# Two buffers for the scan's output matrices, and a new order of the work around layer norm's roots and the powers

## The reference, cut to what matters

```
mod = silu(cond) @ ada_w[i] + ada_b[i]              # shift, scale, gate, three groups of 2048
cn  = rmsnorm(ctx) * (1 + scale) + shift

def chunk_mixer(h):                                  # layer 0
    z = gelu(h @ w_in);  u, v = split(z)
    v = layernorm(v, ln_g, ln_b)                     # mean, squares, root, reciprocal
    return (u * (w_s @ v + b_s)) @ w_out

# layer 1: h[t] = a * h[t-1] + bb @ u[t],  y[t] = real(c @ h[t]), a, bb, c complex, 64 groups
mag = exp(lr * step);  a = mag * (cos, sin)(li * step)
bb  = ((a - 1) * conj(l) / |l|^2) * b
```

## Time and profile before

| | us |
|---|---|
| median of 3 runs | 3821.16 (3813.0, 3821.16, 3826.5) |
| profiled execution, its own time | 3819.04 |
| span of that execution in the trace | 3817.1 |
| first gather of the experts starts, from the span's start | 323.19 |

### The profile page before, as it was taken

How to read it: one execution, slowest core, us unless ns; L and a number is a source line. 1 busy time by engine, 2 the same in 40 slices (tenths; PEclk the granted TensorE clock), 3 DMA queues, 4 the chain that set the end, 5 groups by cost and what they waited for, 6 DMA issues and landing times. The chain is left out here.

```text
span 3817.1 us, 46785 instructions
## 1 busy us (share of the span) xinstructions
PE 3233.0 (85%) x15952; PEld 2126.1 (56%) x15952; DVE 2248.8 (59%) x5038; ACT 1428.4 (37%) x3564; POOL 972.1 (25%) x796
## 2 busy tenths in 40 slices
PE   3877999898889988986748888889769889799897
PEld 2765566454435555532436544444237789577797
DVE  5665667666666666687252576667632289212397
ACT  1222444444344444443242344444432166222265
POOL 0002434333334433444100354445520000000000
PEclk6888999999999999999878999999989999888899
DMA  6747999999999999999684799999952244221353
GB/s 247 284 171 289 421 411 420 421 411 419 420 397 411 410 414 415 413 395 361 272 292 146 294 421 421 421 421 420 410 240 79 79 178 159 116 83 69 126 187 118
DMA packets 177136, 1152.67 MB, mean 302 GB/s; under 512 B 21860, under 2 KB 30264, under 8 KB 43306
## 3 DMA queue, kind: packets, MB, share of 16 engines
q0 software_dynamic: 113936, 827.38, 53.0%
q1 hardware_dynamic: 56058, 304.90, 21.2%
q10 hardware_dynamic: 6944, 17.91, 1.2%
HBM read 1128.86 MB, written 21.25 MB: 301 GB/s over the span
## 5 line engine op out<-in xcount | busy, mean ns | idle before, releaser
L1126 PE MATMUL PS<-AR 128*128 128x512 f32 x3072 | 1508.7, 617 | 257.1 <-ACT AR L1184 248.7
L1311 POOL DMA_INDIRECT AR<-in_peer_uv,AR x768 | 959.0, 1249 | 1507.0 <-PE PS L1126 1097.5
L1287 DVE CUSTOM_DVE_ANT_0 AR<-AR,H 128x1024 f32<-128x1024 f32 x768 | 941.6, 1226 | 664.5 <-DMA AR<-in_peer_uv,AR 644.9
L1126 PEld LDWEIGHTS PS<-AR 128*128 128x128 f32 x3072 | 558.6, 193 | 862.9 <-issue 419.4
L1179 ACT ACTIVATE SM<-SM 128x1 f32<-128x1 f32 x768 | 155.4, 202 | 1152.9 <-DVE SM L1287 1151.7
L1087 PEld LDWEIGHTS PS<-HT,W 128*128 128x128 f32 x1536 | 296.8, 194 | 270.3 <-issue 255.1
L1087 PE MATMUL PS<-HT,W 128*128 128x256 f32 x1536 | 425.0, 385 | 2.7 <-issue 1.3
L1184 ACT ACTIVATE AR<-CON,SM 128x128 f32<-128x128 f32 x768 | 308.4, 402 | 40.3 <-PE PS L1126 15.3
L2576 PE MATMUL PS<-XP,WP 128*128 128x256 f32 x2112 | 264.2, 288 | 22.6 <-DVE WP L2733 15.7
L2576 PEld LDWEIGHTS PS<-XP,WP 128*128 128x128 f32 x2112 | 262.2, 196 | 26.3 <-issue 25.3
L1181 ACT ACTIVATE SM<-SM 128x1 f32<-128x1 f32 x768 | 226.4, 295 | 25.0
(11 more groups left out here) (368 smaller groups left out, 3391.2 us busy)
## 6 DMA issues: line engine op xcount, KB each, us to landing
W<-in_peer_w_q SPq DMA_DIRECT2D x48, 1024.0 KB
W<-in_ada_w SPq DMA_DIRECT2D x32, 1024.0 KB
W<-in_ffn_gate SPq DMA_DIRECT2D x22, 1024.0 KB
W<-in_ffn_val SPq DMA_DIRECT2D x22, 1024.0 KB
W<-in_ffn_out SPq DMA_DIRECT2D x22, 1024.0 KB
W<-in_cm_w_in SPq DMA_DIRECT2D x16, 1024.0 KB
AR<-min_scr SPq DMA_DIRECT2D x16, 1024.0 KB, 10.1
AR<-in_peer_uv,AR POOLq DMA_INDIRECT x768
```

The lines of the kernel that those rows point to most:

```text
L1126: mm = pe.matmul(PS[:, 4 + (u % 2) * 2 + c, :], self.DIAG[:, r % 4, :], self.UV[:, r % RING, D + c * 512:D + (c + 1) * 512], start=(k == 0 ...
L1287: v.tensor_tensor_reduce(rows_, rows_, H[:, self.tb(u), :], 1.0, 0.0, ALU.mult, ALU.add, self.ACTV[:, u % 2, k:k + 1]).then_inc(u_used.sem, 1)
L1311: g.indirect_dma_start(out=self.UV[:, r % RING, :], out_offset=None, in_=t["peer_uv"], in_offset=bass.IndirectOffsetOnAxis(ap=self.IDS[:, ...
```

## The change

The output matrices get a second buffer, at another place of the arena. The second half of `dve_powers` becomes a function of its own, `dve_powers_of`; the first half (a, the factors, bb) is called ahead of the bias of `ada0[0]`, the second half behind it. `act_roots` follows `act_squares`, ahead of `act_in(4)` and `matrices(2)`. ScalarE gets two waits: ahead of each MOUT store but the first for the store before, and ahead of the experts for the store of chunk 6, whose buffer lies where the experts' scores go. The numbers of steps between VectorE's other work are new.

```
-                self.MOUT = view(0, 2, CG, T8 * GDIM)
+                self.MOUT = [view(18432, 2, CG, T8 * GDIM), view(0, 2, CG, T8 * GDIM)]
...   act_store(c)
                 a.wait_ge(self.mout_done, c + 1)
-                a.dma_start(mout_scr[c], self.MOUT.rearrange("p r g x -> p (r g x)")).then_inc(self.mout_out, 16)
+                if c:
+                    a.wait_ge(self.mout_out, c * 16)
+                a.dma_start(mout_scr[c], self.MOUT[c % 2].rearrange("p r g x -> p (r g x)")).then_inc(self.mout_out, 16)
...   dve_powers
                 drain(self.cmul(self.BBR, self.BBI, over_c(self.CO_R), over_c(self.CO_I), self.BR, self.BI, self.T1, self.T2))
+
+            def dve_powers_of(self):
+                L, X1, X2, A_R, A_I, PR, PI = self.link, self.X1, self.X2, self.A_R, self.A_I, self.PR, self.PI
                 L(v.memset(PR[:, 0], 1.0))
...   dve
-                    MIN, CST, MOUT = self.MIN[c % 2], self.CST[c % 2], self.MOUT
+                    MIN, CST, MOUT = self.MIN[c % 2], self.CST[c % 2], self.MOUT[c % 2]
...
-                    if c:
-                        v.wait_ge(self.mout_out, c * 16)
+                    if c > 1:
+                        v.wait_ge(self.mout_out, (c - 1) * 16)
...   first_act
             mixc.act_squares()
+            mixc.act_roots()
             drain(mixc.act_in(4))
             matrices(2)
-            mixc.act_roots()
             drain(mixc.act_in(5))
...
+            a.wait_ge(prep.mout_out, 7 * 16)
             peer0.act(fill_act(), rest_of_matrices, first_block_norm())
...   first_dve
             drain(norm1c.variances())
+            prep.dve_powers()
             ada0[0].add_bias()
-            prep.dve_powers()
+            prep.dve_powers_of()
             matrices = prep.dve()
...
             drain(norm1c.apply())
-            some(40)
+            some(42)
             ada0[1].add_bias()
             mixc.dve_means()
-            some(2)
+            some(1)
             mixc.dve_vars()
-            some(2)
+            some(1)
             drain(mixc.dve_apply(0))
-            some(24)
+            some(30)
             ada0[2].add_bias()
-            some(6)
+            some(4)
             drain(mixc.dve_mix())
```

## The result

| | before | changed |
|---|---|---|
| median of 5 runs | 3824.28 (3813.0 to 3828.56) | 3795.97 (3785.51 to 3800.83) |
| profiled execution, its own time | 3819.04 | 3795.97 |
| span of that execution in the trace | 3817.1 | 3794.2 |
| first gather of the experts | 323.19 | 302.99 |

The forecast was 3798.5 in a range from 3790 to 3809: right in sign and in size. The times that follow are starts from the beginning of the span.

The account below looks back on a forecast made before the run. The prediction took TensorE's ordered list to bound the front and DMA transfers the experts' stretch from the first gather. Gains of 8.46 + 13.12 = 21.6 us gave 3797.5 on the profiled execution, 3799.6 by the median; it said 3798.5, range 3790 to 3809.

Parts of the forecast that it names:

- Part 1, 8.46: First norm on VectorE: with the powers split around the first bias, its application starts at 63.09, not 71.55, gaining 8.46 us.
- The worry about the rows' landing: First norm: the bias 3.08 late might delay the rows' load; landing 2 us later would cut the gain to 6.6.
- The wait of 7.85: TensorE at `prep.pe(3)`: its 7.85 us wait for VectorE's copy ending MIN(3) goes, with 12 us to spare.
- The clock's price, 4.91: `prep.pe(3)` on TensorE: without the wait it runs at the high clock, 6.62 us in place of 11.53.
- The block behind, 0.36: TensorE's block behind `prep.pe(3)`: takes 8.84 us in place of 9.20, gaining 0.36.
- Second buffer and early roots: VectorE and ScalarE before MIN(3): no store wait, roots at 144.1 in place of 164.1 (times of before), 20 us earlier.
- New waits at no cost: ScalarE's waits ahead of MOUT stores and the experts cost nothing; stores 17 us or more apart, 2.8 to spare at the experts.
- Sum, 21.6 at the first gather: Whole front: 8.46 + 13.12 = 21.6 us, putting the first gather at 301.6 in place of 323.19.
- rival (d): TensorE in the front: clock sinks at other places, each `prep` group costing 4.9 more; slower, up to 3831.8; chance 3%.
- signs of being wrong: TensorE's wait for L962 staying, a gather later than 306, or a stretch behind it longer by more than a few us.
- The rest unchanged at 3493.9: From the first gather to the span's end: the distance stays unchanged at 3493.9 us.

Follow-up runs that it names:

- powers_only: The kernel before with only the powers in two parts around the first bias; ratio to before 0.9979, 8.0 us less.
- before_again: The kernel before, unchanged, profiled a second time; first gather at 327.61 us, no ratio given.
- late_roots: The changed kernel with layer norm's roots back behind `matrices(2)`; ratio to before 0.9989, 4.2 us less.
- matrices_only: The changed kernel with the powers joined again behind the first bias; ratio to before 0.9972, 10.7 us less.
- min3_first: late_roots with two more steps of MIN(3) ahead of `dve_apply`, which finish that matrix; ratio to before 0.9970, 11.5 us less.
- after_again: The changed kernel, unchanged, measured and profiled a second time; ratio to before 0.9949, 19.5 us less.
- after_third: The changed kernel, unchanged, profiled a third time; first gather at 307.02 us, no ratio given.
- one_buffer: The changed kernel with a single output buffer again and the last step count between output blocks cut from 3 to 1; ratio to before 0.9976, 9.2 us less.
- roots_only: The kernel before with only layer norm's roots moved right behind the squares; ratio to before 0.9980, 7.6 us less.
- all_three: The changed kernel with chunk 4's and 6's DMA issues moved behind copies, `prep.pe(5)` behind the first output block, and earlier gathers; ratio to before 0.9919, 31 us less.
- tokens_alone: The changed kernel with only the latent tokens' and position rows' loads moved ahead of the first gathers; ratio to before 0.9920, 30.6 us less.
- tokens_early: all_three with the latent tokens' and position rows' loads moved ahead of the first gathers; ratio to before 0.9866, 51 us less.

## Why the prediction was right, step by step

- **Part 1, 8.46.** Measured 8.59 at the application and at the transposes (67.06 against 75.65), and 8.0 by the times of powers_only (interval 1.1 to 14.5). The worry about the rows' landing did not apply: in the kernel before, ScalarE's queue had issued the four stores by 46.35 and GpSimd's load followed 5.9 us later; now they are out by 49.26 and the load follows 2.7 us later, 0.25 earlier than before. The DMA engines' share is 0.99 between 45 and 50 us and 0.42 between 50 and 55 in the trace of before, and 0.98 and 0.45 in the changed one. I read it so that in both the stores landed when the weights ahead of them had; no run tests this. I had passed the lateness on in full.
- **The wait of 7.85.** Gone, as forecast, in all three executions. The size was one draw: it is 9.79 in before_again, and 9.93 in powers_only, where only part 1 is in.
- **The clock's price, 4.91.** `prep.pe(3)` took 6.62, 6.66 and 7.09 in three executions, against 11.53 before. The wait in front of it decides: wait and slow group went and came together in powers_only, late_roots, matrices_only and min3_first. A long wait is not the only thing that makes a group slow, as `prep.pe(7)` with 0.68 ahead of it shows.
- **The block behind, 0.36.** This was one draw. It took 7.15, 8.79 and 10.04 us in the three executions of the changed kernel; these are the rows of after_again and of after_third:

```profile
160.86 8.79 PE L593 MATMUL PS<-W,HT 128*128 128x256 f32 x32
```

```profile
163.10 10.04 PE L593 MATMUL PS<-W,HT 128*128 128x256 f32 x32
```

  The Trainium skill (TensorE: Matmul & The Clock Gate, section "A second HAM failure mode: psum-queue depth-cycling") says that an engine that pauses often between groups of matmuls swings between the two clocks. The traces agree that this block was slowed in two of three executions, and not that it must be; I had read a fixed 8.84 out of it.
- **Second buffer and early roots.** The chain was right (buffer, bias of `ada0[1]`, squares, roots, application, MIN(3)), and for the whole gain both links are needed. The prediction did not say so, and my theory behind it, that the roots did it alone, was wrong: alone they gave 4.7 us (one_buffer) and 6.4 (roots_only) of some 14 at `prep.pe(4)`, in one execution each, and the buffer alone nothing. The roots came at 135.6 as forecast; VectorE idled 6.98 ahead of the means (forecast 7) and 10.2 in the longest wait ahead of the spatial product (forecast 14).
- **New waits at no cost.** So it was: none of ScalarE's new waits shows up ahead of its stores or the experts, though the stores now come as close as 15.8 us (the prediction has 17 or more).
- **Sum, 21.6 at the first gather.** Measured 20.2 in the first trace and 20.3 in the mean. Up to `prep.pe(4)` it was 22.6 in the mean; 3.65 was given back at `prep.pe(7)`. That was rival (d)'s mechanism, at one group and not at five: the clock sank at another place. So the closeness is in part luck. In the first pair of traces the gain at `prep.pe(4)` was 25.0, which is 3.4 more than forecast, because the blocks behind `prep.pe(2)` and `prep.pe(3)` took 7.15 and not 8.84, and `prep.pe(7)` took about as much back. One of the prediction's own signs of being wrong, a gather later than 306, came in one of three executions (307.02), with TensorE's wait gone all the same. By the times, 24.5 and 19.5 us, both intervals hold 21.6 and neither could tell it from 18 or 24.
- **The rest unchanged at 3493.9.** It was 3491.2 in that trace, and 3487.3 and 3483.4 later. I count this as scatter, not as shown.

## What to carry to other kernels

Where an engine runs two strands in turn, look at which instruction inside the other strand's unfinished piece it waits at: finishing the piece first (min3_first), or making the wait end early by freeing all its links, is worth the wait and the slow group behind it. Freeing one link alone moves the stall to the next: it gave a part of the gain at `prep.pe(4)` with the roots (roots_only; in one_buffer it was lost again behind) and nothing with the buffer (late_roots). When the front of a stretch that is paced by transfers gets shorter, ask what is requested only at its start: a load that was issued behind the ring's first gathers arrived 21 to 23 us later here, and 8 when it was issued ahead of it. And read the durations of a stretch with a moving clock from more than one execution before an amount of less than 3 us goes into a sum.

## What the runs showed of the hardware

- The switch of ScalarE's tables costs 1.28 us and nothing more that can be seen. ScalarE's timeline of the changed kernel:

```profile
134.32 1.28 ACT L674 ACT_TABLE_LOAD   x1
135.61 0.30 ACT L674 ACTIVATE SM<-SM 128x1 f32<-128x1 f32 x2
135.93 1.28 ACT L656 ACT_TABLE_LOAD   x1
137.22 0.60 ACT L656 ACTIVATE AR<-PS 128x512 f32<-128x512 f32 x1
```

  The Trainium skill (ScalarE: Activation LUTs, section "What ACT_TABLE_LOAD costs") gives 2.66 us for each, with a drain; here the measurement decides.
- A load of 1 MB that was issued among the first eight gathers of the ring landed 23.3 us later in the changed kernel (issued at 311.17, behind seven of them) and 21.0 in all_three (issued at 302.37, behind all eight). Issued ahead of the gathers it took 7.8 in tokens_alone and 8.0 in tokens_early.
- The same block of 32 matmuls in the same program took between 7.15 and 10.04 us, depending on the execution.
